# RWKV's operands computed in its inputs' stream, a set for each direction, in a two-layer three-mixer block

## What is computed

```python
def rwkv7_mixer(c_s, mu, w0, w_lora_b, a0, a_lora_b, k_k, k_a, r_k, ln_g, ln_b):
    s = centred_shift(c_s, mu)
    r, k, v, codes = jnp.split(s, (WC, 2 * WC, 3 * WC), axis=-1)
    w_code, a_code = ...                       # codes, (b, t, 2 directions, 64) each
    kk = k * k_k, normalized per head
    for d in range(2):
        w = (w0[d] + jnp.tanh(w_code[:, :, d]) @ w_lora_b[d])
        decay = jnp.exp(-jnp.exp(-jax.nn.softplus(-w) - 0.5))
        a = jax.nn.sigmoid(a0[d] + a_code[:, :, d] @ a_lora_b[d])
        k_d = k * (1.0 + (a - 1.0) * k_a)
        # per position, state S of 64 x 64 per head (reverse in time for d == 1)
        #   S = S * w_t + (S @ -kk_t) (kk_t * a_t)^T + v_t k_t^T ;  o_t = S @ r_t
        o = o + rwkv7_scan(r, decay, k_d, v, kk, a, reverse=(d == 1))
        bonus = bonus + jnp.sum(r * k_d * r_k, axis=-1) * v
    return head_groupnorm(o, ln_g, ln_b) + bonus

# layer l of 2:
proj = rmsnorm(x) @ w_in[l]
y_a = hgrn2_mixer(a_q, a_ff, a_fb, a_i, ...) * silu(a_g)
y_b = retention_mixer(b_q, b_k, b_v, ...) * silu(b_g)
y_c = rwkv7_mixer(c_s, ...) * silu(c_g)
mixed = gates[0] * (y_a @ w_branch_a) + gates[1] * (y_b @ w_branch_b) + gates[2] * (y_c @ w_branch_c)
x = x + mixed @ w_out[l]
```

## Time and profile before

| what | value |
|---|---|
| median of 3 runs | 3070.25 us (3069.31 to 3071.65) |
| profiled execution, its own time | 3079.39 us |
| span of the profile | 3077.6 us |
| mean granted clock of TensorE | 0.987 |
| PE busy | 2991.0 us (97%) |
| DVE, ACT, POOL busy | 1665.9 us (54%), 714.8 us (23%), 260.0 us (8%) |
| mixers of layer 0, of layer 1 | about 31 to 942 us, and 993 to 1907 us of the span |
| second block | 1907 us to the end |

### The profile page before, as it was taken

One profiled execution on the slowest core, in us unless ns is written; L12 is line 12 of the kernel. 1 busy time (PEld: TensorE's weight loads), 2 busy tenths in 40 slices (PEclk: granted clock), 3 DMA queues, 4 the chain that ended last, 5 costly groups with the idle time before them and its releaser, 6 DMA issues.

```text
span 3077.6 us, 45154 instructions
## 1 busy us (share of the span) xinstructions
PE 2991.0 (97%) x18944; PEld 2471.2 (80%) x18944; DVE 1665.9 (54%) x3430; ACT 714.8 (23%) x1348; POOL 260.0 (8%) x326
## 2 busy tenths in 40 slices
PE   8999999999999999999999999899999999999999
PEld 7878888888886888788888888796769959766894
DVE  3555557746421553764856431575237767645675
ACT  2333323333111232432433210100121010013100
POOL 1120302103000020120201200000000000000000
PEclk9989999999999998999999999999999999999999
DMA  5332334234343422423323335445334544533443
GB/s 222 126 99 92 93 99 139 81 105 131 111 142 135 146 102 73 129 77 108 113 90 129 92 87 189 146 167 176 129 132 151 167 162 165 173 107 117 151 165 123
DMA packets 153753, 395.55 MB, mean 129 GB/s; under 512 B 90288, under 2 KB 106800, under 8 KB 109648
## 3 DMA queue, kind: packets, MB, share of 16 engines
q1 hardware_dynamic: 51376, 367.94, 34.2%
q10 hardware_dynamic: 100608, 19.93, 3.4%
q0 software_dynamic: 1568, 4.79, 0.4%
HBM read 380.04 MB, written 12.59 MB: 128 GB/s over the span
## 4 chain that ended last, share of the span: by engine, by line
PE 90%; DVE 5%; DMA 3%; ACT 1%; issue 1%; ACTq 0%; DVEq 0%; SPq 0%
PE bank L420 27%; PE bank L1979 18%; PE bank L437 7%; PE bank L1997 7%; PE bank L1802 7%; PE bank L1865 4%; PE bank L1408 2%; PE bank L2008 1%; PE bank L754 1%; PE bank L774 1%; PE bank L912 1%; DMA rw_ex<-x_scratch 1%; PE bank L897 1%; PE bank L995 1%; PE bank L1690 1%; PE bank L926 1%
## 5 line engine op out<-in xcount | busy, mean ns | idle before, releaser
L420 PE MATMUL bank<-h_features,weight_ring 128*128 128x256 f32 x4192 | 965.9, 384 | 2.0 <-DVE h_features L533 1.0
L420 PEld LDWEIGHTS bank<-h_features,weight_ring 128*128 128x128 f32 x4192 | 785.1, 191 | 116.9 <-issue 10.9
L437 PE MATMUL bank<-weight_ring,h_features 128*128 128x256 f32 (+1 forms) x896 | 206.3, 380 | 4.7 <-ACT rt_qk L1707 4.7
L437 PEld LDWEIGHTS bank<-weight_ring,h_features 128*128 128x128 f32 x896 | 164.4, 191 | 28.4 <-ACT rt_qk L1707 6.4
L1979 PE MATMUL bank<-h_features,weight_ring 128*128 128x128 f32 x1408 | 172.0, 275 | 6.1 <-DVE h_features L533 6.1
L1979 PEld LDWEIGHTS bank<-h_features,weight_ring 128*128 128x128 f32 x1408 | 164.3, 192 | 6.9 <-DVE h_features L533 6.9
L2050 ACT COPY mem_normed<-bank 128x128 f32<-128x128 f32 x88 | 23.5, 267 | 481.9 <-PE bank L1979 476.2
L1802 PE MATMUL bank<-y_features,weight_ring 128*128 128x256 f32 x512 | 118.9, 383 | 0.0
L2135 DVE TENSOR_TENSOR mem_normed<-mem_normed,bank 128x256 f32<-128x256 f32 x88 | 37.1, 422 | 130.6 <-PE bank L1979 130.6
L1802 PEld LDWEIGHTS bank<-y_features,weight_ring 128*128 128x128 f32 x512 | 94.3, 190 | 12.8 <-issue 0.7
L1979 PE MATMUL bank<-h_features,y_hgrn_features 128*128 128x128 f32 x704 | 93.0, 275 | 0.0
(11 more groups left out here) (543 smaller groups left out, 4941.3 us busy)
## 6 DMA issues: line engine op xcount, KB each, us to landing
weight_ring<-in_w_in SPq DMA_DIRECT2D x146, 1024.0 KB, 5.0
weight_ring<-in_f00w SPq DMA_DIRECT2D x33, 1024.0 KB, 4.8
weight_ring<-in_f01w SPq DMA_DIRECT2D x33, 1024.0 KB, 4.9
weight_ring<-in_f10w SPq DMA_DIRECT2D x33, 1024.0 KB, 4.9
weight_ring<-in_f11w SPq DMA_DIRECT2D x33, 1024.0 KB, 4.8
weight_ring<-in_w_b SPq DMA_DIRECT2D x16, 1024.0 KB, 4.9
weight_ring<-in_w_out SPq DMA_DIRECT2D x16, 1024.0 KB, 4.9
weight_ring<-in_conv_in SPq DMA_DIRECT2D x10, 1024.0 KB, 4.9
```

Source lines behind the costliest of these rows:

```text
L420: m = e.matmul(bank[:, j, :], w[:, k, j * P:(j + 1) * P], x[:, k, :], start=k == 0, stop=k == kt - 1, skip_group_check=True)
L437: m = e.matmul(bank[:, t * n:(t + 1) * n], x[:, k, t * P:(t + 1) * P], w[:, k, :], start=k == 0, stop=k == kt - 1, skip_group_check=True)
```

## The change

The units' operands (part 1 above) leave R and go to P, the stream of the inputs. P now runs, for each quarter, the inputs and then the operands of both directions (`ahead`), in bank 3 instead of banks 1 and 2. With it:

- `sig`, `bm`, `ex`, `kr`, `tot`, `mid`, `phi` are there once for each direction (`rwkv_direction`), the bonus once for each of two quarters. `a` and `kd` stay single: the second code's sigmoid waits for the unit before to have transposed its keys ("tok"), the first code's for the output of the unit two before.
- The decay's chain starts once the first code's sigmoid is done, before `kd`.
- The keys' transposes and their copies move from behind the first step's output to behind the scores.
- POOL clears `scored_a` and `scored_k` once the unit before has made its last output, in every unit (before, in the first direction, after the whole quarter had ended); it loads the low-rank weights once the second direction's products have read them. The state is cleared once, at the start.
- The centred squares of the head norm use `vt` as scratch instead of `kr`. Retention's DVE waits for its own first rotation before the second. The program is built with `dynamic_dma_scratch_size=4096`.
- The order strings of the mixers are new for all five engines. TensorE's instructions are the same ones in another order.

```diff
@@ ORDER, one of ten strings (first lines)
     ("mixers0", "tensor"):
-        "R P4 R4 H P4 H2 P4 H2 P5 H P H P H5 P H P4 H3 R P R P R P R3 P H6 B2 P4 R H R3 P R2 P R2 P R P2 R H2 B "
+        "R P4 H2 P4 H2 P4 H2 P5 H P H P H4 P2 H P H P2 H P H3 R P H R H3 B R B R B R4 B2 H P4 B4 H2 B P R H2 R3 P "
...
+def rwkv_operands_pe(e, g, l, q, d):
+    S, R = g.ri, g.R
+    for code in range(2):
+        yield
+        bank = pairs(g.banks.take(S, "lora", l, q, d, code))
+        for free in g.banks.free("lora", l, q, d, code):
+            e.wait_ge(*free)
+        if d == 0 and code == 0:
+            e.wait_ge(g.lora_sem, 32 * (4 * l + q + 1))
+            e.wait_ge(*g.cd.act.at("tanh", l))
...
+def rwkv_operands_act(e, g, l, q, d):
+    for code, out, bias in ((0, Z.sig, f"w0{d}{l}"), (1, R.a, f"a0{d}{l}")):
+        yield
+        e.wait_ge(*S.pe.at("lora", l, q, d, code))
+        before = unit - (2 if code == 0 else 1)
+        if before >= 0:
+            B = (before // 8, before // 2 % 4, before % 2)
+            e.wait_ge(*(g.rw.pe.at("o", *B, 1) if code == 0 else g.rw.pe.at("tok", *B, 1)))
...
+def ahead(inputs, operands, e, g, l):
+    for q in range(4):
+        yield from inputs(e, g, l, q)
+        for d in range(2):
+            yield from operands(e, g, l, q, d)
...
 def rwkv_pe(e, g, l):
-            for code in range(2):
-                yield
-                bank = pairs(g.banks.take(S, "lora", l, q, d, code))
...
                 if c == d:
-                    e.wait_ge(*dve.at("ops", l, q, d))
+                    e.wait_ge(*g.ri.dve.at("ops", l, q, d))
...
+            cs = slice(0, P) if d == 0 else slice(P, T)
+            for i, src in enumerate((R.kd, R.a)):
+                yield
+                bank = g.banks.take(S, "tok", l, q, d, i)
...
 def rwkv_pool(e, g, l):
-        if q:
-            e.wait_ge(*S.dve.at("end", l, q - 1))
...
-        e.memset(R.state, 0.0).then_inc(*S.pool.up("state", l, q))
         for d in range(2):
+            yield
+            if d == 0 and q == 0:
+                if l:
+                    e.wait_ge(*g.ri.pe.at("lora", l - 1, 3, 1, 1))
+                lora_pool(e, g, l, 0)
+            if d and q < 3:
+                e.wait_ge(*g.ri.pe.at("lora", l, q, 1, 1))
+                lora_pool(e, g, l, q + 1)
             yield
             if d:
                 e.wait_ge(*S.pe.at("o", l, q, 0, 1))
-                e.wait_ge(g.rw_scores_sem, 32 * ((4 * l + q) * 2 + 1))
+            elif q:
+                e.wait_ge(*S.pe.at("o", l, q - 1, 1, 1))
...
             e.memset(R.scored_a, 0.0).then_inc(*S.pool.up())
             e.memset(R.scored_k, 0.0).then_inc(*S.pool.up("scored", l, q, d))
```

More of the change, by code:

```diff
@@ L764, in doublings_pe @@
             for i, rows in parts:
-                m = e.matmul(bank[rows, i], R.xT[rows, i, :], level_half(R.prod, lv, d)[rows, i], start=True,
+                m = e.matmul(bank[rows, i], Z.xT[rows, i, :], level_half(Z.prod, lv, d)[rows, i], start=True,
                              stop=True, skip_group_check=True)
@@ L773, in doublings_pe @@
         for i, rows in parts:
-            m = e.matmul(bank[rows, i], R.prod[rows, i, :], level_half(R.xT, lv, 1 - d)[rows, i], start=True,
+            m = e.matmul(bank[rows, i], Z.prod[rows, i, :], level_half(Z.xT, lv, 1 - d)[rows, i], start=True,
                          stop=True, skip_group_check=True)
@@ L873, in rwkv_inputs_dve @@
     yield
+def rwkv_operands_pe(e, g, l, q, d):
[8 more added lines that the diff above has]
+            e.wait_ge(*g.cd.act.at("tanh", l))
+        for n in range(2):
+            m = e.matmul(bank[:, n, :], R.lora[code][d * 64:(d + 1) * 64, n * P:(n + 1) * P],
+                         g.codes[d * 64:(d + 1) * 64, code, :], start=True, stop=True, skip_group_check=True)
+        m.then_inc(*S.pe.up("lora", l, q, d, code))
+    yield
@@ new lines, in rwkv_operands_act @@
+def rwkv_operands_act(e, g, l, q, d):
+    S, R, Z = g.ri, g.R, g.R.of[d]
+    dve, act, unit = S.dve, S.act, (4 * l + q) * 2 + d
+    for code, out, bias in ((0, Z.sig, f"w0{d}{l}"), (1, R.a, f"a0{d}{l}")):
[5 more added lines that the diff above has]
+            e.wait_ge(*(g.rw.pe.at("o", *B, 1) if code == 0 else g.rw.pe.at("tok", *B, 1)))
+        bank = pairs(g.banks.get("lora", l, q, d, code))
+        for n in range(2):
+            s = e.activation(out[:, n, :], bank[:, n, :], ACT.Sigmoid, bias=g.col(bias, 2 * q + n))
+        s.then_inc(*act.up("lora", l, q, d, code))
+        g.banks.empty(act, "lora", l, q, d, code)
+    yield
+    e.wait_ge(*dve.at("phi", l, q, d))
+    e.activation(Z.sig, Z.sig, ACT.Exp, scale=-DECAY).then_inc(*act.up("prev", l, q, d))
+    e.activation(Z.ex, Z.bm, ACT.Exp, scale=-DECAY).then_inc(*act.up("here", l, q, d))
+    e.wait_ge(*act.now())
+    e.activation(Z.bm, Z.bm, ACT.Exp, scale=DECAY).then_inc(*act.up("back", l, q, d))
+    e.activation(Z.phi, Z.phi, ACT.Exp, scale=-DECAY).then_inc(*act.up("phi", l, q, d))
+    yield
@@ new lines, in rwkv_operands_dve @@
+def rwkv_operands_dve(e, g, l, q, d):
+    S, R, Z = g.ri, g.R, g.R.of[d]
+    dve, act, bonus = S.dve, S.act, g.R.bonus[q % 2]
+    r, k, _, kk, _ = R.inputs[q % 2]
+    bm3, sig3 = (z.rearrange("p n (c s) -> p (n c) s", c=TT) for z in (Z.bm, Z.sig))
+    yield
+    e.wait_ge(*act.at("lora", l, q, d, 0))
+    for n in range(2):
+        v = e.tensor_tensor_scan(Z.bm[:, n, :], g.const("scan"), Z.sig[:, n, :], 0.0, ALU.mult, ALU.add)
+    v.then_inc(*dve.up())
+    e.wait_ge(*dve.now())
+    e.tensor_copy(Z.tot.unsqueeze(2), bm3[:, :, P - 1:P]).then_inc(*dve.up())
+    yield
+    e.wait_ge(*dve.now())
+    if d == 1:
+        e.tensor_tensor(bm3, Z.tot.unsqueeze(2).to_broadcast([P, 4, P]), bm3, ALU.subtract).then_inc(*dve.up())
+        e.wait_ge(*dve.now())
+        e.tensor_tensor(bm3, bm3, sig3, ALU.add).then_inc(*dve.up())
+    e.tensor_scalar(Z.mid, Z.tot, 0.5, None, ALU.mult).then_inc(*dve.up())
+    e.wait_ge(*dve.now())
+    e.tensor_tensor(bm3, bm3, Z.mid.unsqueeze(2).to_broadcast([P, 4, P]), ALU.subtract).then_inc(*dve.up())
+    e.wait_ge(*dve.now())
+    e.tensor_tensor(sig3, bm3, sig3, ALU.subtract).then_inc(*dve.up())
+    mid2 = Z.mid.rearrange("p (n c) -> p n c", c=TT)
+    e.tensor_tensor(Z.phi, mid2[:, :, 0], mid2[:, :, 1], ALU.add).then_inc(*dve.up("phi", l, q, d))
+    yield
+    e.wait_ge(*act.at("lora", l, q, d, 1))
+    e.wait_ge(*dve.at("kk", l, q))
+    for n in range(2):
+        v = e.tensor_scalar(R.kd[:, n, :], R.a[:, n, :], 1.0, g.col(f"k_a{l}", 2 * q + n), ALU.subtract, ALU.mult)
+    v.then_inc(*dve.up())
+    e.wait_ge(*dve.now())
+    e.scalar_tensor_tensor(R.kd, R.kd, 1.0, k, ALU.add, ALU.mult).then_inc(*dve.up())
+    e.scalar_tensor_tensor(R.a, R.a, -1.0, kk, ALU.mult, ALU.mult).then_inc(*dve.up())
+    yield
+    e.wait_ge(*dve.now())
+    if d == 0:
+        e.tensor_tensor(bonus, r, R.kd, ALU.mult).then_inc(*dve.up())
+    else:
+        z = view(flat(Z.kr[:, 0]), (2, T))
+        e.tensor_tensor(z, r, R.kd, ALU.mult).then_inc(*dve.up())
+        e.wait_ge(*dve.now())
+        e.tensor_tensor(bonus, bonus, z, ALU.add).then_inc(*dve.up())
+    yield
+    e.wait_ge(*act.at("prev", l, q, d))
+    e.wait_ge(*dve.now())
+    e.tensor_tensor(Z.kr[:, :, :, 0, :], chunked(kk), chunked(Z.sig), ALU.mult).then_inc(*dve.up())
+    yield
+    e.wait_ge(*act.at("here", l, q, d))
+    e.tensor_tensor(Z.kr[:, :, :, 1, :], chunked(r), chunked(Z.ex), ALU.mult).then_inc(*dve.up())
+    yield
+    e.wait_ge(*act.at("back", l, q, d))
+    e.tensor_tensor(R.kd, R.kd, Z.bm, ALU.mult).then_inc(*dve.up())
+    e.tensor_tensor(R.a, R.a, Z.bm, ALU.mult).then_inc(*dve.up("ops", l, q, d))
+    yield
@@ L930, in rwkv_pe @@
                             m.then_inc(*pe.up("scored_k", l, q, d, c, par))
+            cs = slice(0, P) if d == 0 else slice(P, T)
+            for i, src in enumerate((R.kd, R.a)):
+                yield
+                bank = g.banks.take(S, "tok", l, q, d, i)
+                for free in g.banks.free("tok", l, q, d, i):
+                    e.wait_ge(*free)
+                for n in range(2):
+                    m = e.transpose(bank[:, n * P:(n + 1) * P], src[:, n, cs], eye)
+                m.then_inc(*pe.up("tok", l, q, d, i))
             for step, c in enumerate((0, 1) if d == 0 else (1, 0)):
                 W = (l, q, d, step)
-                cs = slice(c * P, (c + 1) * P)
                 yield
@@ L999, in rwkv_pe @@
                 if step == 0:
-                    for i, src in enumerate((R.kd, R.a)):
-                        yield
-                        bank = g.banks.take(S, "tok", *W, i)
-                        for free in g.banks.free("tok", *W, i):
-                            e.wait_ge(*free)
-                        for n in range(2):
-                            m = e.transpose(bank[:, n * P:(n + 1) * P], src[:, n, cs], eye)
-                        m.then_inc(*pe.up("tok", *W, i))
                     yield
@@ L1027, in rwkv_pe @@
```

(28 more changed lines are left out.)

179 lines of the change are left out of this document (65 added, 114 removed), and 104 rows, old and new, of the table ORDER.

## The result

| | before | after |
|---|---|---|
| first comparison, median (range) | 3070.95 us (3069.31 to 3072.24, 4 runs) | 3054.25 us (3052.44 to 3057.14, 4 runs) |
| second comparison, made later (the run after_again) | 3078.93 us (3070.86 to 3085.59, 14 runs) | 3053.02 us (3049.63 to 3055.08, 4 runs) |
| profiled execution | 3079.39 us, clock 0.987 | 3052.44 us, clock 0.994 |

The change makes the kernel faster. The ratio to the kernel before is 0.9939 (95% interval 0.9927 to 0.9951) in the first comparison and 0.9917 (0.9902 to 0.9932) in the second. 3054.25 lies inside my range, but the gain was forecast at 41 us, and it is 17 to 26.

What follows compares the result with a forecast made beforehand. TensorE, 97% busy, bounds the kernel; it loses 34.8 us idle and 29 to the clock, 64 in all. Keeping 16 of waits and 7 of clock gains 41: 3079.4 − 41 − 9.1 = 3029 us, range 3008 to 3064.

Steps and rivals of the forecast that it cites:

- 1, operands leave the chain: RWKV operands computed a unit earlier, 58 to 75 us of TensorE work ahead of use in five of eight units.
- 2, the fill goes to the inverse: Freed projection matmuls cover the inverse's DMA return; waits for x and xT gone, −19.2 us, bounds 0 to −19.2.
- 3, the low-rank weights: Loaded after their last reader, so L897's 3.5 us go; 3.2 us kept for products sharing bank 3, bounds 0 and 8.
- 4, unit 0: Each layer's first unit has only 10.4 us of projections over its operand chain; 4 us of waits kept, bounds 0 and 16.
- 5, POOL's clears: Clears wait for each unit's last output, delaying DVE's masks; 4 us kept, bounds 0 and 29; clears can also stall DVE.
- 6, retention and HGRN2: Waits on retention's rotation (3.3 us) and HGRN2's finish (3.9) go; the rotated keys' 4.7 us stay.
- 7, the clock: Both long clock falls (−17.7 us) and two of five short ones go with the waits; about 7 us of loss kept.
- the signs that I named: L759's x wait under 3 us, mixers' idle under 20, clock 0.95 or above, 1 to 3 us waits at L1011 and L892.
- A: Mixer waits move: 30 to 35 us of idle return in small pieces, only long clock falls won; 3052 or 3061; chance 0.15.
- B: No change: TensorE was not waiting for RWKV's chain, other streams' waits fill the time; 3064 to 3076 us; chance 0.08.
- C: Slower: HGRN2's round trips come late in 24 places, 48 us of waits plus clock falls; 3088 us; chance 0.15.

Runs made afterwards that it cites:

- after_again: The changed kernel run once more with no edit, on the chip of the later runs: 3053.02 us.
- place1: The changed kernel with 16 projection matmuls (6.9 us) of unit (q=0, d=1) put back behind its first doubling, in both layers: 3081.14 us.
- rkb_tt: The changed kernel with the bonus multiplied by r_k in the operands, as a tensor_tensor with the factor broadcast: 3037.99 us.
- rkb_early: The changed kernel with the bonus multiplied by r_k in the operands' last step, not behind the last output, still a tensor_scalar: 3034.35 us.

## Why the prediction was wrong

The forecast was 3029 us, the measurement 3054.25: 25.2 us. Two steps failed. 10.9 us are the first, 14.0 the second, and 0.3 is rounding (3079.4 − 41 is 3038.4, where the sum has 3038.3, and less 9.1 it is 3029.3).

**The step from the profiled execution to the median: 10.9 us.** I took 9.1 us off because the profiled execution lay that far over the median of the three runs shown. I treated it as an offset. It was part of the loss: the kernel before falls to the lower clock by a different amount in each execution, those three runs lay at the low end of what it does (medians of 3078.10, 3078.93 and 3074.03 us in the larger samples; that the chip has a part in it can't be excluded), and the executions that I had worked on were typical. The changed kernel's profiled execution is 1.8 us under its median. 9.1 + 1.8 = 10.9. That the first comparison shows 17 us of gain and the second 26 is the same: the changed kernel's medians are 1 us apart, those of the kernel before 8. On its own scale my sum of 41 is compared with 3079.39 − 3052.44 = 27.0 us.

**The sum itself: 14.0 us too high.** By its steps:

- *1, operands leave the chain:* right. There is no wait at L892, and none for operands at L1011.
- *2, the fill goes to the inverse:* right. 19.2 us forecast, 18.8 measured, with little to spare: in the three runs without the bonus wait, x is waited for once, 2.4 to 3.1 us, in the unit at 375 us. place1 shows what a unit's fill is worth.
- *3, the low-rank weights:* the 3.5 us went. The 3.2 us that I kept for bank 3 did not come.
- *4, unit 0:* I kept 4 us and measured nothing.
- *5, POOL's clears:* this is the step that failed. I had both facts: the clears move right behind the last output, and a clear stalls a DVE instruction for its own length. I then priced it at "4 us in all", for the masks, and left the second price in a sentence without asking which DVE instructions stand in that place and who waits for them. The masks lost nothing that shows. L1308 stands there, it is a `tensor_scalar` like L1304, and TensorE needs it 2 us later: 12.9 us of waits. With the 1.8 us behind L1328 the step cost 14.7 us of idle. The upper bound of 29 us held it, the value that I took did not. Without the 12.9 us the kernel is 15 us (rkb_tt) to 19 us (rkb_early) faster.
- *6, retention and HGRN2:* rotation and finish went as forecast. The 4.7 us of the rotated keys, which I kept, fell to 0.8. In their place came 2.8 us at HGRN2's scales, 2.6 at L802 and 1.1 at L1101.
- *7, the clock:* 7 us forecast, and the windows 1150 to 1200 and 1200 to 1250 (0.90 and 0.97) make 6.5. Right in size.

In the mixers the waits left add up to 22 us instead of my 16. With 6.5 of the clock, 64 − 29 = 35 us should have been gained in the profile, and 27 were. Some 3 of the other 8 us lie behind the mixers: a short fall behind layer 0's that was not there before, and a longer one behind layer 1's. The other 5 are missing in TensorE's busy time, where the clock's share should show. From each layer's first projections to its output projection, TensorE's busy time adds up to 1804.0 us before (897.5 and 906.5) and 1786.7 after (890.3 and 896.4). It fell by 17.3 us, where 29 − 6.5 = 22.5 were to come from the clock; no row shows why, and this stays open. In layer 0, where the idle time hardly changed, these 7.2 us of busy time are nearly all that the change gained.

Of the signs that I named, two came: no wait of L759 for x, and a clock of 1.00 from 200 to 250. Three did not: the idle time is 22 us and not under 20, the clock at that place of layer 1 is 0.90, and there is no wait at L892 nor one for operands at L1011.

**The rivals.** A came nearest in time (3052 to 3061) but only half in kind: 22 us of waits and not 30 to 35, and more than half of them one wait that came back seven times from one cause. B is wrong. C is wrong here: HGRN2's round trips cost 2.8 us, not 48, though place1 shows that they are next in line as soon as fill is taken away.

The version that multiplies the bonus early runs at 3034.35 us and beats both kernels: it is the change with its largest new wait removed. That my forecast of 3029 us lies near it is partly luck. Its profiled execution gains 46.5 us on the profile before, more than my 41, and the 9.1 us that I took off besides were no offset.

## What to carry to other kernels

When work of one engine moves, list what its neighbours run at that moment, not only who waits for the moved work: here clears on POOL show no wait of their own and cost 15 to 19 us through a DVE multiplication that is held beside them, and the cure is to compute that factor earlier or with another kind of instruction. Where every engine has a fixed order, moving fill on one of them moves the copies of its results on another, and a chain may stand behind these. Don't correct a profile by its distance to a few medians before knowing the kernel's spread; here the kernel that lost more time to the clock spread more.

## What was not expected of the hardware

- The clock's falls differ between executions of the same instructions. The second block is the same code in all runs; in place1's profiled execution its window of 2700 to 2900 had a granted clock of 0.93, in the nine other profiles 1.00. That is 28 us at the half level, so 14 us lost, and this execution lay 9 us over the median of its run.
- A short wait can be followed by a fall too: the changed kernel waited no longer than 1.4 us at a scale product in front of layer 1's doublings, and the clock was 0.90 over 1150 to 1200. Behind 1.1 us at the same place (rkb_early) it was 1.00.
